# Attention output transposed in PSUM, the first convolution norm placed inside the attention, probabilities scaled before they are transposed

## The chip, the cores and the metric

The kernel runs on one core of a Trainium2 chip. Its engines are TensorE (PE, with PEld for its loads of weights), VectorE (DVE), ScalarE (ACT), GpSimd (POOL) and SyncE (SP), which issues the loads from memory. The metric is the device time of one execution in microseconds (us).

## The reference, cut to what matters

One layer of a decoder for a prompt of 1024 tokens and a sample group of 32 tokens (8 x 4), 1024 channels. What the change touches is the first part:

```python
q, k, v, a, gate = jnp.split(rms_norm(x, g_pre_mix) @ w_in, ...)
# 8 heads x 64; three dilated windows, combined by their softmax denominators
attn = combine_branches(outs, lses).reshape(B, T, 512)
c = causal_dwconv(a * sigmoid(gate), conv_w) + conv_b      # 512 channels, width 31
c = silu(layer_norm(c, ln_conv_g, ln_conv_b))              # the first norm of c
mix = concat([rms_norm(attn, g_out_attn), rms_norm(c, g_out_conv)])   # the second norm of c
x = x + rms_norm(mix @ w_out, g_post_mix)
```

Cross-attention into 256 memory tokens and a gated ConvFFN follow. All inputs and outputs are float32.

## The kernel before, in words

Activations are held transposed, channels on the partitions and 1056 tokens as columns, and the projections run over three tile columns of 352 tokens each, in the order 2, 0, 1 (CONV_ORDER). Each projection is a row of units: one unit is one weight tile of 1024 x 128 through one tile column. A weight tile is loaded by SP into one of four slots (`raw`), split by ACT into a high part (`whi`, `split_to`) and by DVE into a low part (`wlo`, `low_to`); three products of high and low parts make one float32 product. The output projection, the cross-attention's query and its output are the NX = 72 units of the loop over `t`; the first of them is the first unit spoken of below.

Each engine works through its queue in the order in which the program writes it; waits are on semaphores (`mark` counts up, `at` waits). The attention is a loop over steps s, the same on all engines. A step is a block of 128 queries i (0 to 7) and a pair of heads hp (0 to 3), 32 steps, i slowest, with (i + 1) x 128 keys. The three dilated windows are one softmax with a bias. A step is spread over the loop: `scores(s, 0)` and `maxima(s, 0)`, for more than 512 keys a second part, `negate(s)` and the exponentials `probabilities(s)` on ACT, in place in `Pp`; at s + 1 TensorE transposes the probabilities (`turn_p`), ACT copies them to `PT` (`turned`), and DVE takes the reciprocal of the sums (`shares`); at s + 2 TensorE multiplies (`product`) and DVE scales the result by the reciprocals into `ATT` (`attended`). Between them stand the slots of the sample group (`sample(g, r)`, three a step from s = 2 to 31, 44 for each of two groups of four batches): key tiles of the cache are transposed through bank 5 and multiplied (r = 0 to 27), a softmax, then four window products (r = 35, 37, 39, 41) on four groups of 32 columns of the array.

In the product, the transposed probabilities are the stationary operand (128 x 128) and V's columns of both heads the moving one; of each result one half is used:

```python
ins = mm(bank[4][:, e * P:(e + 1) * P], PT[:, e, blk * P:(blk + 1) * P],
         V[:, blk, hp * P:(hp + 1) * P], blk == 0, blk == i)
```

ATT has tokens on the partitions. Behind the attention stands the work between it and the output projection. For the convolution: means over channels by a matmul with ones (`conv_mean`), subtraction (`conv_centre`), squares (`conv_squares`), their mean (`conv_square_mean`), root (`conv_root`), reciprocal and scaling (`conv_scale`), silu, and squares, mean, root and scaling once more for the second norm. For the attention: sums of squares by row (`attention_square`), root, reciprocal, nine diagonal matrices DGA, and the transposition with scaling in one matmul (`turn_att`), before the first unit for tile column 2, behind units 0 to 3 for column 0 and behind units 8 to 11 for column 1. `mix_low` makes the high and low parts for the projection (`op_hi`, `op_lo`). The first weight tiles of the output projection are split partly at the end of the input projection and partly at step 24 (ACT) and 26 (DVE).

Of the kernel before, what the change touches and what calls it, by code (L numbers as in the profile page):

```python
# [130 lines left out]
def layout(nc, ctx, A, O, counts):  # L131
# [70 lines left out]
    DGA = [mn(f"DGA{i}", 61440 + 512 * i, [P, P]) for i in range(TT + 1)]  # L202
# [7 lines left out]
    ATT = mn("ATT", 20480, [P, TT + 1, AW])  # L210
# [9 lines left out]
    attsT = mn("attsT", 140288, [P, AT, NS])  # L220
# [17 lines left out]
    SQ = [mn(f"SQ{i}", 129024 + 1408 * i, [P, CW]) for i in range(4)]  # L238
    op_hi = [mn(f"op_hi{i}", 67584 + 22528 * i, [P, NT, CW], F32R) for i in range(2)]
# [148 lines left out]
    def y_free(eng, name, c):  # L388
# [3 lines left out]
        if (name, c) == ("out", 0):  # L392
            eng.wait_ge(*at("csq_used", 2 * CH * CT - 1))
        elif (name, c) == ("out", 1):
# [166 lines left out]
    def _(act):  # L561
# [136 lines left out]

        def sample(g, r):

            if 0 <= r < GROUP and on_scalar(g * GROUP + r):
# [37 lines left out]
        def attention_square(i):  # L739
            n = P if i < TT else NS  # L740
            if i == 0:
                act.wait_ge(*at("cst_out", BD - 1))
            else:
                act.wait_ge(*at("ass", i - 1))
            act.wait_ge(*at(*(("att", (AT * i + AT - 1, 1)) if i < TT else ("att8", 0))))
            act.activation(junk[0:n, :], ATT[0:n, i, :], ACT.Square, accum_out=ssx[0:n, i, 0:1]).then_inc(*mark("ass", i))
# [22 lines left out]
        for i in range((LAST_STEP - 6) // 4 + 1, TT):  # L769
            attention_square(i)  # L770

        attention_square(TT)
        act.wait_ge(*at("ass", TT))
        act.activation(rx2[:, 0:9], ssx[:, 0:9, 0], ACT.Sqrt, bias=eps[:, :], scale=1.0 / AW).then_inc(*mark("asd", 0))

        def conv_squares(second, j):
            c = CONV_ORDER[j]
            for k in range(CT):
                n = (second * CH + j) * CT + k
                act.wait_ge(*at("cs" if second else "cc", (c, k)))  # L780
                if n >= 4:
                    act.wait_ge(*at("csq_used", n - 4))
                act.activation(SQ[n % 4][:, :], C[:, k, c * CW:(c + 1) * CW], ACT.Square).then_inc(*mark("csq", n))

# [1496 lines left out]
```

## Time and profile before

| | |
|---|---|
| median of 3 runs | 1888.34 us (1885.1 to 1892.19) |
| the profiled execution | 1887.06 us, its span 1885.3 us |
| mean granted clock of TensorE | 0.982 |
| PE busy | 1794.4 us, 95% of the span |
| DVE busy | 1104.6 us, 59% |
| ACT busy | 869.7 us, 46% |

The span goes from the first to the last instruction. The attention lies at about 336 to 591 us of it, the first unit of the output projection starts at 631.89 us. A busy TensorE in these tables may still be waiting for its own pipeline, since the ends of matmuls are modelled.

### The profile page before, as it was taken

What the parts mean: (1) busy time and instruction counts of PE and PEld (TensorE: products, weight loads), DVE (VectorE), ACT (ScalarE), POOL (GpSimd) and SP (SyncE); (2) the same over time, 40 slices, a digit from 0 to 9 for tenths busy, and PEclk for the clock granted to TensorE, in tenths of its full rate; (3) what the DMA queues carried; (4) which work ended last, traced back from release to release, by engine and by line L of the source; (5) the groups of instructions that cost most, each with busy time, mean ns of one, the idle gap of its engine ahead of it and who ended that gap; (6) DMA issues with size and microseconds to landing.
All of it is one profiled execution on the core that took longest, in us unless ns stands there. A gap on an engine that the chain in (4) does not pass through costs nothing.

```text
span 1885.3 us, 30869 instructions
## 1 busy us (share of the span) xinstructions
PE 1794.4 (95%) x12354; PEld 1667.8 (88%) x12354; DVE 1104.6 (59%) x2055; ACT 869.7 (46%) x1647; POOL 0.9 (0%) x10
## 2 busy tenths in 40 slices
PE   7999999789998799999999898999999999999998
PEld 7999999556776689898877898999999999999998
DVE  5499993344445547753456756764467543576633
ACT  6322222244445456655445645544454543555533
POOL 0000000000000000000000000000000000000000
PEclk9999999899999799999999999999999999999999
DMA  7132122335231145444444333444444544444543
GB/s 234 56 122 80 56 91 91 141 125 190 79 119 51 36 122 162 147 142 129 134 145 124 105 108 112 134 134 139 141 135 134 165 131 138 135 140 140 152 138 101
DMA packets 349220, 233.76 MB, mean 124 GB/s; under 512 B 7979, under 2 KB 322465, under 8 KB 349071
## 3 DMA queue, kind: packets, MB, share of 16 engines
q1 hardware_dynamic: 342907, 220.24, 38.5%
q10 hardware_dynamic: 6172, 11.55, 1.7%
q8 instruction: 99, 1.62, 0.4%
q14 instruction: 42, 0.34, 0.1%
HBM read 220.68 MB, written 11.50 MB: 123 GB/s over the span
## 4 chain that ended last, share of the span: by engine, by line
PE 84%; DVE 7%; ACT 6%; issue 2%; DMA 1%; ACTq 0%; SPq 0%; DVEq 0%
PE bank L1134 78%; PE bank L1131 6%; ACT whi L570 1%; DVE wlo L1721 1%; DVE op_lo L1708 1%; DVE Y L1708 1%; ACT wide L584 1%; DVE op_x L2036 1%; DVE cv L1708 1%; DVE XT L2033 0%; ACT KTS L706 0%; DVE Sx L2021 0%; DVE KTS L1886 0%; DMA raw<-in_w_out_dram 0%; DMA stage_p<-in_ln_conv_b_dram 0%
## 5 line engine op out<-in xcount | busy, mean ns | idle before, releaser
L1134 PE MATMUL bank<-op_hi,whi 128*128 128x352 f32 x1632 | 542.8, 333 | 5.8 <-ACT Y L866 2.3
L1134 PE MATMUL bank<-op_hi,wlo 128*128 128x352 f32 x1632 | 528.3, 324 | 0.0
L1134 PE MATMUL bank<-op_lo,whi 128*128 128x352 f32 x1632 | 527.7, 323 | 0.0
L1721 DVE TENSOR_TENSOR wlo<-raw,whi 128x1024 fp32r<-128x1024 f32 (+1 forms) x312 | 373.6, 1200 | 260.0 <-ACT whi L570 259.4
L570 ACT ACTIVATE whi<-raw 128x1024 fp32r<-128x1024 f32 (+1 forms) x312 | 325.2, 1043 | 301.8 <-PE bank L1134 102.9
L1134 PEld LDWEIGHTS bank<-op_hi,whi 128*128 128x128 f32 x1632 | 309.9, 190 | 15.1 <-issue 10.5
L1134 PEld LDWEIGHTS bank<-op_lo,whi 128*128 128x128 f32 x1632 | 311.3, 191 | 0.3
L1134 PEld LDWEIGHTS bank<-op_hi,wlo 128*128 128x128 f32 x1632 | 309.7, 190 | 0.0
L1134 PE MATMUL bank<-fhi,whi 128*128 128x352 f32 x528 | 171.2, 324 | 0.0
L1134 PE MATMUL bank<-fhi,wlo 128*128 128x352 f32 x528 | 170.8, 323 | 0.0
L1134 PE MATMUL bank<-h1hi,whi 128*128 128x352 f32 x480 | 157.2, 327 | 3.0 <-DVE h1lo L1708 3.0
L1708 DVE SCALAR_TENSOR_TENSOR C<-U,cw,C 128x1024 f32<-128x1024 f32 x120 | 154.1, 1284 | 3.7
L1134 PE MATMUL bank<-h1hi,wlo 128*128 128x352 f32 x480 | 155.0, 323 | 0.0
L1134 PE MATMUL bank<-h1lo,whi 128*128 128x352 f32 x480 | 154.9, 323 | 0.0
L1134 PEld LDWEIGHTS bank<-fhi,wlo 128*128 128x128 f32 x528 | 99.8, 189 | 0.0
L1134 PEld LDWEIGHTS bank<-fhi,whi 128*128 128x128 f32 x528 | 99.4, 188 | 0.0
L1134 PEld LDWEIGHTS bank<-h1hi,whi 128*128 128x128 f32 x480 | 90.8, 189 | 3.1 <-DVE h1lo L1708 3.1
L1134 PEld LDWEIGHTS bank<-h1lo,whi 128*128 128x128 f32 x480 | 91.0, 190 | 0.0
L1134 PEld LDWEIGHTS bank<-h1hi,wlo 128*128 128x128 f32 x480 | 90.8, 189 | 0.0
L1134 PEld LDWEIGHTS bank<-V,PT 128*128 128x128 f32 x576 | 67.1, 192 | 22.0 <-issue 21.1
L1134 PE MATMUL bank<-flo_a,whi 128*128 128x352 f32 x264 | 84.9, 322 | 0.0
L1708 DVE SCALAR_TENSOR_TENSOR cv<-aext,fw,cv 128x352 f32<-128x352 f32 (+2 forms) x176 | 81.0, 491 | 3.9
(273 smaller groups left out, 2371.3 us busy)
## 6 DMA issues: line engine op xcount, KB each, us to landing
raw<-in_w_up_dram SPq DMA_DIRECT2D x132, 512.0 KB, 3.8
raw<-in_w_down_dram SPq DMA_DIRECT2D x48, 512.0 KB, 3.6
raw<-in_w_out_dram SPq DMA_DIRECT2D x24, 512.0 KB, 3.6
raw<-in_w_xq_dram SPq DMA_DIRECT2D x24, 512.0 KB, 3.6
raw<-in_w_xo_dram SPq DMA_DIRECT2D x24, 512.0 KB, 3.6
raw<-in_w_in_dram SPq DMA_DIRECT2D x20, 512.0 KB, 3.7
raw<-in_w_down_dram SPq DMA_DIRECT2D x24, 384.0 KB, 3.2
cached<-in_cache_win_k_dram SPq DMA_DIRECT2D x8, 1024.0 KB, 5.5
```

What stands on the lines that cost most here:

```text
L570: act.activation(whi[v % SLOTS][:, 0:nk, :], raw[v % SLOTS][:, 0:nk, :], ACT.Copy).then_inc(*mark("w_hi", v))
L584: act.activation(wide[0:n, :], src, ACT.Square, accum_out=ssx[0:n, i, 0:1]).then_inc(*mark("xss", i))
L1131: return pe.transpose(out, in_, ident[r:r + n, r:r + n])
L1134: return pe.matmul(out, lhsT, rhs, start=first, stop=last)
L1708: return dve.scalar_tensor_tensor(out=out, in0=in0, scalar=scalar, in1=in1, op0=op0, op1=op1)
L1721: dve.tensor_tensor(wlo[v % SLOTS][:, 0:nk, :], raw[v % SLOTS][:, 0:nk, :], whi[v % SLOTS][:, 0:nk, :].bitcast(F32), ALU.subtract).then_in ...
L2036: dve.tensor_tensor(op_x[SLOT[name, c]][:, m, :], XT[c][:, m, :], r[:, :], ALU.mult).then_inc(*mark("opx", (name, c, m)))
```

## The change

In the attention the operands of the product change places: V's 64 columns of one head are stationary, the transposed probabilities move, and the two heads write partitions 0 to 63 and 64 to 127 of one bank, in turn for each block. The output has channels on the partitions. So the reciprocals can no longer be applied to it by row; DVE multiplies the probabilities in place instead, after the next step's first maxima, and the transposes wait for that. ATT becomes [128, 4, 1056], the sample's outputs go straight into its last 32 columns, and the row sums, the diagonals and `turn_att` go. The attention's norm is now made like the convolution's: squares on ACT, mean by ones on TensorE, root on ACT, reciprocal and scaling on DVE, for tile column 2 ahead of the first unit, for the others behind units 2 and 3.

The first norm of the convolution moves into sample slots: means and centring into group 0's slots r = 29 to 34, squares, square means, roots and scaling into group 1's r = 28 to 35, all through bank 5. Its buffers SQ1, STD1 and RSC1 lie in the high halves of the four weight slots. So no weight tile of the output projection is split until step 30 (ACT) and 31 (DVE), where all four are.

```diff
+    halves = [place(f"half{i}", RING + 8192 * (i // 2) + 4096 + 1408 * (i % 2), [P, CW]) for i in range(8)]
+    SQ1, STD1, RSC1 = halves[0:4], halves[4:6], halves[6:8]
...
-            split_to(u + 3)
+            split_to(min(u + 3, LAST_IN))
...
+            if g == 1 and r - GROUP - 2 in (0, 2, 4):
+                conv_root(0, (r - GROUP - 2) // 2)
+            if g == 1 and r - GROUP in (0, 2, 4):
+                conv_squares(0, (r - GROUP) // 2)
...
-            if s >= 6 and (s - 6) % 4 == 0:
-                attention_square((s - 6) // 4)
...
-            if s == NP - 8:
+            if s == NP - 2:
                 split_to(XFIRST + 3)
...
+        def att_squares(j):
+            c = CONV_ORDER[j]
+            act.wait_ge(*at("att", NP - 1))
+            act.wait_ge(*at("satt", (1, 3, 1)))
+            for k in range(AT):
+                n = j * AT + k
+                if n >= 4:
+                    act.wait_ge(*at("asq_used", n - 4))
+                act.activation(SQA[n % 4][:, :], ATT[:, k, c * CW:(c + 1) * CW], ACT.Square).then_inc(*mark("asq", n))
+
+        def att_root(j):
+            act.wait_ge(*at("asq_used", j * AT + AT - 1))
+            if j:
+                act.wait_ge(*at("ars", j - 1))
+            act.activation(STDA[:, :], bank[5 - j % 2][:, 0:CW], ACT.Sqrt, bias=eps[:, :]).then_inc(*mark("asd", j))
+
         conv_silu(0)
         conv_squares(1, 0)
+        att_squares(0)
         conv_silu(1)
         conv_silu(2)
+        att_root(0)
         conv_root(1, 0)
...
-                pe.wait_ge(*at("pexp", (s, e)))
+                pe.wait_ge(*at("pn", (s, e)))
                 take(2 + e, "pt", (s, part, e))
...
-            take(4, "att", (s, 1))
+            take(4, "att", s)
             for e in range(2):
                 pe.wait_ge(*at("pt", (s, parts_of(i) - 1, e)))
-                for blk in range(i + 1):
-                    ins = mm(bank[4][:, e * P:(e + 1) * P], PT[:, e, blk * P:(blk + 1) * P], V[:, blk, hp * P:(hp + 1) * P], blk == 0, blk == i)
+            for blk in range(i + 1):
+                for e in range(2):
+                    h = 2 * hp + e
+                    ins = mm(bank[4][64 * e:64 * e + 64, 0:P], V[:, blk, h * DH:(h + 1) * DH], PT[:, e, blk * P:(blk + 1) * P], blk == 0, blk == i)
...
+            if g == 0 and r - GROUP in (1, 3, 5):
+                conv_mean((r - GROUP) // 2)
+            if g == 1 and r - GROUP in (1, 3, 5):
+                conv_square_mean(0, (r - GROUP) // 2)
...
+        def att_mean(j):
+            b = 5 - j % 2
+            take(b, "asd", j)
+            for k in range(AT):
+                n = j * AT + k
+                pe.wait_ge(*at("asq", n))
+                mm(bank[b][:, 0:CW], ones_c[:, :], SQA[n % 4][:, :], k == 0, k == AT - 1).then_inc(*mark("asq_used", n))
...
-            if t in range(AT):
-                turn_att(0, t)
-            if t - 8 in range(AT):
-                turn_att(1, t - 8)
+            if t in (2, 3):
+                att_mean(t - 1)
...
+            if g == 0 and r - GROUP - 2 in (0, 2, 4):
+                conv_centre((r - GROUP - 2) // 2)
+            if g == 1 and r - GROUP - 3 in (0, 2, 4):
+                conv_scale(0, (r - GROUP - 3) // 2)
...
             dve.reciprocal(prden[:, s % 2, :], pden[:, s % 2, :]).then_inc(*mark("prd", s))
+            dve.wait_ge(*at("prd", s))
+            n = (STEPS[s][0] + 1) * P
+            for e in range(2):
+                dve.tensor_scalar(Pp[s % 2][:, e, 0:n], Pp[s % 2][:, e, 0:n], prden[:, s % 2, e:e + 1], None, ALU.mult).then_inc(*mark("pn", (s, e)))
...
-                dve.tensor_scalar(ATT[:, i, h * DH:(h + 1) * DH], bank[4][:, e * P + e * DH:e * P + e * DH + DH], prden[:, s % 2, e:e + 1], None, ALU.mult).then_inc(*mark("att", (s, e)))
+            dve.tensor_copy(ATT[:, hp, i * P:(i + 1) * P], bank[4][:, 0:P]).then_inc(*mark("att", s))
 
         for s in range(LAST_STEP + 1):
             if s < NP:
                 maxima(s, 0)
+            if 0 <= s - 1 < NP:
+                shares(s - 1)
             if 0 <= s - 2 < NP:
                 attended(s - 2)
             sample(*sample_slot(s, 0))
-            if 0 <= s - 1 < NP:
-                shares(s - 1)
...
-            if s == NP - 6:
+            if s == NP - 1:
                 low_to(XFIRST + 3)
...
+        def att_scale(j):
+            c = CONV_ORDER[j]
+            dve.wait_ge(*at("asd", j))
+            dve.reciprocal(RSCA[j][:, :], STDA[:, :]).then_inc(*mark("ars", j))
+            dve.wait_ge(*at("ars", j))
+            for k in range(AT):
+                cols = ATT[:, k, c * CW:(c + 1) * CW]
+                dve.tensor_tensor(cols, cols, RSCA[j][:, :], ALU.mult).then_inc(*mark("an", (c, k)))
+
+        att_scale(0)
         conv_scale(1, 0)
...
-            if t - 1 in range(AT):
-                mix_low(0, t - 1)
+            if t in (2, 3):
+                att_scale(t - 1)
+            if t in (3, 4):
+                for k in (0, 1):
+                    mix_low(0, 2 * (t - 3) + k)
```

`mix_low` reads ATT in place of bank 4 or 5, as it reads C.

## Rows read from the trace of the kernel before

**Rows 1.** Page, part 4: the chain that ended last, by engine

```profile
PE 84%; DVE 7%; ACT 6%; issue 2%; DMA 1%; ACTq 0%; SPq 0%; DVEq 0%
```

**Rows 2.** Windows: length, busy us of PE, PEld, DVE, ACT, POOL, clock, DMA

```profile
370.00:380.00 10.00, 8.18 (x86) 5.43 (x79) 4.61 (x15) 3.97 (x14) 0.00 (x0) 1.00 0.21 60
560.00:590.80 30.80, 29.83 (x328) 24.62 (x327) 9.76 (x40) 15.53 (x29) 0.00 (x0) 1.00 0.13 46
590.80:631.90 41.10, 27.63 (x94) 17.71 (x92) 29.13 (x54) 25.76 (x51) 0.00 (x0) 0.76 0.18 58
666.00:672.00 6.00, 6.00 (x31) 5.92 (x29) 1.25 (x2) 0.61 (x2) 0.00 (x0) 0.72 0.42 109
```

**Rows 3.** The costliest group of 336 to 591 us: count, busy, mean ns

```profile
L1134 PE MATMUL bank<-V,PT 128*128 128x128 f32 x576 | 73.2, 282 | 2.5 <-ACT PT L737 2.5
```

**Rows 4.** Timeline of a late step: start us, duration us, engine, line

```profile
562.08 1.13 ACT L729 ACTIVATE Pp<-Pp,pneg 128x1024 f32<-128x1024 f32 x1
...
562.20 1.13 PE L1134 MATMUL bank<-KT,QT 64*128 64x512 f32 x4
...
563.26 3.84 PE L1134 MATMUL bank<-V,PT 128*128 128x128 f32 x32
...
566.94 1.04 PE L1131 MATMUL bank<-ident,Pp 128*128 128x128 f32 x8
...
568.96 1.74 PE L1134 MATMUL bank<-cached,PTS 128*32 128x128 f32 x56
...
569.74 0.75 DVE L1712 CUSTOM_DVE_ANT_0 Pp<-bank,wt,pmx 128x512 f32<-128x512 f32 x1
...
570.63 0.42 PE L1134 MATMUL bank<-V,PTS 32*32 32x128 f32 x8
...
570.98 1.09 PE L1131 MATMUL bank<-ident,Pp 128*128 128x128 f32 x8
...
572.00 1.13 PE L1134 MATMUL bank<-KT,QT 64*128 64x512 f32 x4
```

**Rows 5.** Timeline from the attention's last steps to the first unit

```profile
586.32 1.09 ACT L737 ACTIVATE PT<-bank 128x512 f32<-128x512 f32 x2 [0.32 <-PE bank L1131]
...
590.71 0.60 PE L1131 MATMUL bank<-ident,attsT 128*32 128x128 f32 x4
...
591.15 7.26 PE L1134 MATMUL bank<-C,ones_c 128*128 128x352 f32 x24
...
605.00 1.64 ACT L783 ACTIVATE SQ<-C 128x352 f32<-128x352 f32 x4
...
613.98 4.67 ACT L797 ACTIVATE C<-C,prm 128x352 f32<-128x352 f32 x8
...
618.66 1.28 ACT L790 ACT_TABLE_LOAD   x1
...
620.54 2.35 DVE L1983 RECIPROCAL RSC<-STD 128x352 f32<-128x352 f32 x1 [4.91 <-ACT STD L790]
622.93 1.83 DVE L1987 TENSOR_TENSOR C<-C,RSC 128x352 f32<-128x352 f32 x4
...
631.89 0.63 PE L1134 MATMUL bank<-op_hi,whi 128*128 128x352 f32 x1 [1.85 <-DVE op_lo L1708]
```

**Rows 6.** Groups of VectorE in the whole span, by shape

```profile
L1721 DVE TENSOR_TENSOR wlo<-raw,whi 128x1024 fp32r<-128x1024 f32 x288 | 350.7, 1220 | 246.3 <-ACT whi L570 245.6
...
L1997 DVE TENSOR_SCALAR DGA<-ident,rx 128x128 f32<-128x128 f32 x9 | 1.8, 277 | 0.0
...
L1903 DVE TENSOR_SCALAR Ps<-Ps,rden 128x928 f32<-128x928 f32 x2 | 1.4, 703 | 0.1
```

**Rows 7.** Timeline of TensorE behind the first unit; in brackets the wait

```profile
653.53 0.91 PE L1134 MATMUL bank<-DGA,ATT 128*128 128x128 f32 x6 [1.41 <-DVE op_lo L1708]
...
665.68 0.46 PE L1131 MATMUL bank<-ident,xtok 64*128 64x64 f32 x4 [2.53 <-DVE op_lo L1708]
```

**Rows 8.** The same at the ninth unit

```profile
685.70 1.41 PE L1134 MATMUL bank<-DGA,ATT 32*128 32x32 f32 x8
```

More of the change, by code:

```diff
@@ L811, in mix_low @@
             s = SLOT["mix", c]
[L812 to L813 removed]
+            act.wait_ge(*at("an", (c, m)))
+            act.activation(op_hi[s][:, m, :], ATT[:, m, c * CW:(c + 1) * CW], ACT.Copy, scale=g_of("g_out_attn", m)).then_inc(*mark("op_hi", ("mix", c, m)))
             act.wait_ge(*at("cf", (c, m)))
@@ L1362, in window_product, with conv_mean, conv_square_mean @@
             ins.then_inc(*mark("spv", b))
+        def conv_mean(j):
+            c = CONV_ORDER[j]
+            pe.wait_ge(*at("conv", "end"))
+            take(5, "cc", (c, CT - 1))
+            for k in range(CT):
+                ins = mm(bank[5][:, 0:CW], ones_c[:, :], C[:, k, c * CW:(c + 1) * CW], k == 0, k == CT - 1)
+            ins.then_inc(*mark("cmean", c))
+        def conv_square_mean(second, j):
+            b = (6, 1, 0)[j] if second else 5
+            take(b, "csd", second * CH + j)
+            for k in range(CT):
+                n = (second * CH + j) * CT + k
+                pe.wait_ge(*at("csq", n))
+                mm(bank[b][:, 0:CW], ones_c[:, :], (SQ if second else SQ1)[n % 4][:, :], k == 0, k == CT - 1).then_inc(*mark("csq_used", n))
         def sample(g, r):
+            if g == 0 and r - GROUP in (1, 3, 5):
+                conv_mean((r - GROUP) // 2)
+            if g == 1 and r - GROUP in (1, 3, 5):
+                conv_square_mean(0, (r - GROUP) // 2)
             if r == 0:
@@ L1596, in key_rows @@
             ins.then_inc(*mark("mkx_t", (mt, hf)))
-        for m in range(AT):
-            if m == 2:
-                conv_square_mean(1, 0)
-            turn_att(2, m)
+        conv_square_mean(1, 0)
+        att_mean(0)
         for t in range(NX):
@@ L1877, in _, with conv_centre, conv_scale @@
         dve.wait_ge(*at("tables", "s"))
+        def conv_centre(j):
+            c = CONV_ORDER[j]
+            dve.wait_ge(*at("cmean", c))
+            for k in range(CT):
+                cols = C[:, k, c * CW:(c + 1) * CW]
+                dve.tensor_tensor(cols, cols, bank[5][:, 0:CW], ALU.subtract).then_inc(*mark("cc", (c, k)))
+        def conv_scale(second, j):
+            c, n = CONV_ORDER[j], second * CH + j
+            dve.wait_ge(*at("csd", n))
+            r = RSC[:, j, :] if second else RSC1[n % 2][:, :]
+            dve.reciprocal(r, (STD if second else STD1)[n % 2][:, :]).then_inc(*mark("crs", n))
+            dve.wait_ge(*at("crs", n))
+            for k in range(CT):
+                cols = C[:, k, c * CW:(c + 1) * CW]
+                dve.tensor_tensor(cols, cols, r, ALU.mult).then_inc(*mark("cf" if second else "cn", (c, k)))
         def sample(g, r):
+            if g == 0 and r - GROUP - 2 in (0, 2, 4):
+                conv_centre((r - GROUP - 2) // 2)
+            if g == 1 and r - GROUP - 3 in (0, 2, 4):
+                conv_scale(0, (r - GROUP - 3) // 2)
             if 0 <= r < GROUP and not on_scalar(g * GROUP + r):
@@ L2138, in _ @@
                 conv_scale(1, t + 1)
-            if t - 1 in range(AT):
-                mix_low(0, t - 1)
+            if t in (2, 3):
+                att_scale(t - 1)
+            if t in (3, 4):
+                for k in (0, 1):
+                    mix_low(0, 2 * (t - 3) + k)
             if t - 8 in range(AT):
```

124 lines of the change are left out of this document (25 added, 99 removed).

## The prediction

> **What bounds the kernel now.** First I read the chain that ended last: 84% of it is TensorE's work [rows 1]. So time is won where TensorE waits or where its own work shrinks, and an edit on VectorE or ScalarE costs something only where TensorE ends up waiting for it. Then the windows. The attention runs from 336 to 590.7 us. Early in it TensorE is 82% busy (8.18 of 10 us from 370), in its last 30.8 us 97%. Behind it comes the hole that this change is about: from 590.8 to 631.9 us TensorE is busy 27.6 of 41.1 us, at a mean granted clock of 0.76, before the first unit of the output projection starts [rows 2]. The groups of the attention show the product of PT and V as TensorE's largest work there, 576 records [rows 3]. The timeline of a late step shows the order: first scores, product, transposes, second scores, sample work, transposes, and from one step's first scores to the next's it is 572.00 - 562.20 = 9.80 us [rows 4].
>
> **The product, values stationary.** 32 records take 566.94 - 563.26 = 3.68 us until the next instruction starts, 0.115 us each [rows 4]; 576 of them are 66 us. The number of records and their 128 moving columns stay the same, but each now fills only 64 columns of the array, the lower and the upper 64 in turn. Nothing in the trace has that shape. Two rows are near. 56 records of the sample's window product, on four groups of 32 columns in turn, take 570.63 - 568.96 = 1.67 us, 0.030 each, a quarter of 0.115: groups of columns run side by side, even into one bank. And four score records of 512 columns, on the two halves of the rows in turn, take 563.26 - 562.20 = 1.06 us [rows 4], where a record of 352 columns alone takes 0.293 (below), so four of 512 in a row would take 1.7. So I take half of 0.115: 33 us instead of 66, a gain of 33.1. The other bound is 0.115, no gain, and beyond it the 0.282 of a record by itself [rows 3].
>
> The handover from the 32-column products to the full transposes (570.63, then 570.98, with 8 records between) shows no gap [rows 4], so I take nothing for the change of shape. The Trainium skill (TensorEngine Tiling (Array Packing), Key Properties) says that changing the tiling mode drains the engine. By the row the sum stays as it is, by the rule it is the drain among the rivals.
>
> **The convolution norm, moved into the attention.** Three means and three square means, 24 records of 352 columns each, leave the hole. 24 take 7.26 us less the last one's tail of 0.2, 0.293 each [rows 5], so 48 of them bring TensorE +14.1 us. With the product that makes -33.1 + 14.1 = -19.0 us of TensorE's work in the attention. DVE gets 12 subtractions, 12 multiplications and three reciprocals of 2.35 us; ACT gets 12 squares and three roots. A root needs another table than the exponentials, each load takes 1.28, so up to six loads or 7.7 us of ACT [rows 5].
>
> **The probabilities scaled on DVE, in place.** Each step gets two multiplications of (i + 1) x 128 columns. Rows of that form are 277 ns at 128 columns and 703 at 928, so 754 at 1024, and 33 us of busy time over the 64. Upper bound for 1024: the 1220 of an operation with two tensors [rows 6]. In return two small multiplications of the output become one copy. DVE is 32 to 46% busy in the attention [rows 2], so its sum costs nothing; the order does. The transposes of step s now wait for exponentials, reciprocal and scaling. The chain of a step at i = 7: two exponentials 2.3 us, two scalings 1.4, the second head's transposes 0.5, second scores 1.06, two maxima 1.4, and about 1.4 for the accumulator reads, the reciprocal, the negation and seven handovers: 8.1 us [rows 4, 6]. TensorE's own work in such a step falls from 9.8 to 8.0 us. So the two are even, and from there a shorter product gives nothing.
>
> **What of the 19 us shows.** I laid the orders of the queues side by side with these durations. Steps 0 to 11 (i = 0 to 2): the product gives 4 x 0.23 x 6 = 5.5 us, but TensorE already waits there, and the longer way through DVE (0.15 + 2 x 0.3 us a step) takes it all: 0. Steps 12 to 15: -3.7 for the product, +7.05 for the means, +2.7 since bank 5 is held until DVE has centred four tiles and the sample's key transposes queue behind it: +6.0. Steps 16 to 23: 10.1 on paper, 8.3 kept. Steps 24 to 27: -6.4, +7.05, and +3 for TensorE waiting on squares and roots behind table loads: +3.7. Steps 28 to the end: -7.4, and +4.0 since the splitting of the first four weight tiles (ACT a little less, DVE 1.22 us each [rows 6]) now stands in the last two steps, ahead of the last exponentials and the last scaling: -3.4. Sum -2.0 us. Bounds: -19 if every wait hides; +12 if a scaling takes 1.22 us, when the chain is 9.1 us a step.
>
> **The hole.** Now: 590.71 to 631.89, 41.2 us. After, counted from the end of the last product: ACT is free 3.3 us before (587.41), loads a table (1.28), applies silu to one tile column (half of 4.67; ends at +0.4), squares it (1.64, +2.0), squares the attention's (1.64, +3.7), silu for two columns (4.67, +8.4), loads the root's table (1.28, +9.7), root (+10.1). DVE: reciprocal 2.35 and four multiplications 1.83 for the attention (+14.3), the same for the convolution (+18.5), eight low parts at 0.46 as the multiplications (+22.2), and 1.8 for the first ACT copies and the handovers: 24 us [rows 5]. Gone are the first conv passes, nine diagonals and the transposing matmuls. Gain 41.2 - 24.0 = 17.2 us. TensorE still stands idle ahead of the first unit, so that unit's slow start stays (a record of 0.63 us at 631.89) [rows 5].
>
> **Behind the hole.** The transposes of the attention for the other two tile columns go: four times 0.8 us (6 records) and four times 1.3 (8 records), 8.4 us [rows 7, 8]. Two attention means come: 2 x 2.3 = 4.6. Their waits go too: 1.41 us at 653.53 and 2.53 at 665.68, and behind the latter the granted clock is 0.72 for 6 us, 1.7 us lost [rows 2, 7]. Together 3.8 + 3.9 + 1.7 = 9.4. ACT's two roots now hold its queue for TensorE's means after the third and fourth unit, and the copies and splits behind them, so I keep 7.0. The low parts are due at the ninth unit and come some 7 us ahead of it.
>
> **Sum.** -2.0 - 17.2 - 7.0 = -26.2 us. The profiled execution took 1887.06 (span 1885.3), 1.3 below the median of 1888.34, so 1862 us.
>
> **Rivals.**
> Product without overlap: the two halves of the columns run one after another at 0.115. For it: no row has the shape. Against: both neighbours overlap. The attention then grows by the 14.1 of the conv and some 7.4 of waits, +21.5 instead of -2.0: 1886 us, no change.
> Halves that wait for each other, the case on the other side: if the weights of one half can't be loaded while the other half runs, a record costs more than 0.115. The sum is zero near 0.119 and slower by 0.5% (9.4 us) from 0.135; at the 0.282 of a record by itself it is 1886 + 576 x 0.167 = 1982 us. Against it: with four groups of columns the loads hide [rows 4].
> The clock: TensorE will wait 1 to 2 us several times a step at the end of the attention. The granted clock fell behind the pause of 2.53 us at 665.68, yet held at 1.00 with 82% busy from 370 [rows 2, 7]. Half clock for 20 us costs 10: 1872.
> A drain at each product: the rest of a record by itself, 0.282 - 0.115 = 0.17 us, once more a step than now, 32 x 0.17 = 5 us: 1867.
> A dearer scaling: at 1.22 us the attention grows 12 us instead of shrinking 2: 1876.
>
> **Chances.** Likeliest 0.62, its own range 1850 to 1871; clock 0.10; drain 0.05; scaling 0.08; no overlap 0.09; halves waiting 0.06. Range 1849 to 1880. Less than 0.5% (9.4 us) can't be told from no change: faster 0.82, same 0.12, slower 0.06.
>
> **What would show it.** Product records 0.058 us apart; the last product ending near 589; 24 us from there to the first unit; transposes waiting for DVE's Pp; no matmul reads ATT as weights. It is wrong if the records stay 0.115 apart, if the granted clock is 0.50 inside the attention, or if the conv work holds the sample work up by more than 10 us.

## The result, and the profile after

The changed kernel took 1868.36 us (median of 4 runs, 1866.86 to 1871.51) against 1886.87 us of the kernel before on the same chip (median of 4; the 1888.34 further up is that of the first three): ratio 0.9899, 95% interval 0.9874 to 0.9924. The forecast was 1862 us, range 1849 to 1880. The profiled execution's span is 1867.3 us, 18.0 below that of before.

The chain that ended last, by engine, in the changed kernel's page (beside [rows 1]):

```profile
PE 83%; DVE 8%; ACT 5%; issue 3%; DMA 1%; ACTq 0%; SPq 0%; DVEq 0%
```

Windows of the changed kernel, columns as in [rows 2]; the second is the attention's end, the third the hole:

```profile
412.00:450.00 38.00, 29.86 (x392) 20.52 (x393) 17.66 (x55) 10.95 (x27) 0.00 (x0) 0.91 0.48 165
560.00:595.50 35.50, 28.91 (x408) 20.21 (x396) 21.41 (x56) 23.45 (x40) 0.00 (x0) 1.00 0.24 83
595.50:619.30 23.80, 5.09 (x19) 3.01 (x17) 12.54 (x20) 17.24 (x34) 0.00 (x0) 0.72 0.29 100
666.00:672.00 6.00, 6.00 (x44) 5.96 (x43) 1.75 (x2) 2.83 (x8) 0.00 (x0) 1.00 0.37 106
```

TensorE was 97% busy at the end of the attention before, and is 81% busy there now (28.91 of 35.5 us). The hole has shrunk from 41.1 to 23.8 us. The slow stretch at 666 us is gone. The stretch from 412 us had 35.30 us of TensorE's work and a clock of 1.00 before; now it has 29.86 and 0.91.

The product as a group, and a late step on the timeline (beside [rows 3, 4]):

```profile
L1144 PE MATMUL bank<-PT,V 128*64 128x128 f32 x576 | 38.8, 279 | 2.8 <-ACT PT L761 2.8
```

```profile
567.78 1.13 PE L1144 MATMUL bank<-KT,QT 64*128 64x512 f32 x4
568.84 1.97 PE L1144 MATMUL bank<-PT,V 128*64 128x128 f32 x32
571.17 1.32 PE L1141 MATMUL bank<-ident,Pp 128*128 128x128 f32 x8 [0.36 <-DVE Pp L1966]
572.42 1.13 PE L1144 MATMUL bank<-KT,QT 64*128 64x512 f32 x4
...
577.58 1.97 PE L1144 MATMUL bank<-PT,V 128*64 128x128 f32 x32
```

32 records take 1.97 us with the last one's tail of some 0.2, so 0.057 us each: the two column halves run side by side. The mean duration is the same as before (279 against 282 ns), and yet the busy time has fallen from 73.2 to 38.8 us: what halved is the distance between records, not the time one spends in the engine. The transposes now wait for DVE's `Pp`.

From the last product to the first unit (beside [rows 5]):

```profile
593.63 1.97 PE L1144 MATMUL bank<-PT,V 128*64 128x128 f32 x32 [0.78 <-ACT PT L761]
...
600.19 4.66 ACT L788 ACTIVATE C<-C,prm 128x352 f32<-128x352 f32 x8
604.87 1.28 ACT L805 ACT_TABLE_LOAD   x1
606.16 0.55 ACT L805 ACTIVATE STDA<-bank,eps 128x352 f32<-128x352 f32 x1
...
606.82 2.35 DVE L1995 RECIPROCAL RSCA<-STDA 128x352 f32<-128x352 f32 x1 [10.88 <-ACT STDA L805]
...
619.28 0.63 PE L1144 MATMUL bank<-op_hi,whi 128*128 128x352 f32 x1 [16.58 <-DVE op_lo L1708]
```

The last product ends at 595.5, not at 589 as forecast; the first unit follows 23.8 us later, forecast 24.0. The wait to read here is DVE's 10.88 us for STDA: ACT sits on two columns of silu ahead of the root.

What TensorE waits for inside the attention, changed kernel, 402 to 600 us; columns: what waits, for what, us in total, times, longest:

```profile
PE bank L1141 <- DVE Pp L1966: 6.4, 7, 1.8
PE bank L1144 <- ACT half L710: 3.7, 2, 2.3
...
PE bank L1144 <- DMA cached<-in_cache_win_v_dram: 2.6, 1, 2.6
...
PE bank L1144 <- DVE C L1884: 1.5, 1, 1.5
```

None of the first, second and fourth were there before; the third was 1.2 us.

### The profile page after: what moved, and what is told of

Its sections match the earlier page's. It is cut to its first block, busy times and chain, and to the rows that moved or that the text cites. A ratio compares the mean times of both kernels' runs of the same rounds, so it can differ in the third digit from the quotient of the medians.

```text
span 1867.3 us, 30727 instructions
## 1 busy us (share of the span) xinstructions
PE 1757.9 (94%) x12286; PEld 1623.9 (87%) x12286; DVE 1134.5 (61%) x2091; ACT 876.4 (47%) x1648; POOL 0.9 (0%) x10
## 4 chain that ended last, share of the span: by engine, by line
PE 83%; DVE 8%; ACT 5%; issue 3%; DMA 1%; ACTq 0%; SPq 0%; DVEq 0%
PE bank L1144 77%; PE bank L1141 6%; DVE wlo L1721 1%; ACT whi L574 1%; DVE op_lo L1708 1%; DVE Y L1708 1%; DVE XT L2035 1%; ACT wide L588 1%; DVE Sx L2023 1%; DVE op_x L2038 0%; ACT KTS L730 0%; ACT Pp L753 0%; DVE KTS L1907 0%; DVE Sy L2016 0%; DVE Pp L1966 0%
## 5 line engine op out<-in xcount | busy, mean ns | idle before, releaser
L2016 DVE TENSOR_TENSOR Sy<-Sy,SQy 128x352 f32<-128x352 f32 x63 | 33.0, 523 | 79.3 <-ACT SQy L834 79.3
```

The source lines that it names most:

```text
L2016: dve.tensor_tensor(Sy[:, :], Sy[:, :], SQy[:, :], ALU.add).then_inc(*mark("ysum", (name, c, m)))
```

## The experiments

Every kernel is taken apart by three marks of TensorE's timeline: the first scores (near 338 us), the start of the last product, and the first unit. The two stretches between them (the last product counts to the hole here), and what follows the first unit ("rest"), are in the table, in us; what lies ahead of the first scores, 336 to 339 us, is left out; "ratio" is to the kernel before on the same chip.

| | attention | hole | rest | median | ratio |
|---|---|---|---|---|---|
| before | 249.8 | 44.8 | 1253.4 | | 1 |
| changed | 255.8 | 25.7 | 1248.0 | 1868.36 | 0.9899 |
| changed, again | 253.5 | 25.7 | 1247.2 | 1868.25 | 0.9901 |
| heads in turn | 262.1 | 25.7 | 1248.2 | 1875.03 | 0.9941 |
| conv norm behind | 241.3 | 45.4 | 1249.9 | 1876.14 | 0.9943 |
| scaling ahead | 255.3 | 25.7 | 1248.3 | 1868.08 | 0.9904 |
| split in pauses | 250.9 | 25.7 | 1250.2 | 1866.70 | 0.9894 |
| silu behind roots | 254.9 | 22.2 | 1249.1 | 1864.93 | 0.9885 |
| centring at once | 250.7 | 25.7 | 1250.1 | 1866.35 | 0.9890 |
| three together | 251.4 | 22.2 | 1246.0 | 1862.09 | 0.9871 |
| unscaled | 248.4 | 25.7 | 1248.7 | 1862.21 | 0.9858 |
| unscaled, conv behind | 229.6 | 45.4 | 1248.6 | 1862.72 | 0.9859 |
| three, scaled on GpSimd | 355.8 | 22.3 | 1250.7 | 1969.02 | 1.0428 |
| three, scaling ahead | 256.0 | 22.9 | 1248.0 | 1864.60 | 0.9876 |

The rest spreads from 1246 to 1251 over kernels that are the same there, and the attention by 2.3 us between two executions of the same kernel: smaller differences in one row say nothing. The hole repeats to 0.15 us wherever ACT's order there is the same, except in the last kernel.

The attention once more, cut at the first scores of steps 12, 16, 24 and 28; its last stretch ends where the last product starts:

| | to step 12 | 12 to 15 | 16 to 23 | 24 to 27 | from 28 |
|---|---|---|---|---|---|
| before | 73.2 | 26.5 | 67.3 | 37.4 | 45.5 |
| changed | 71.7 | 36.8 | 60.0 | 42.3 | 45.0 |
| changed, again | 70.5 | 35.5 | 61.0 | 40.9 | 45.5 |
| conv norm behind | 69.0 | 29.7 | 61.7 | 37.7 | 43.3 |
| split in pauses | 70.6 | 33.8 | 60.0 | 40.9 | 45.6 |
| centring at once | 71.5 | 32.5 | 60.0 | 40.9 | 45.8 |
| unscaled | 70.2 | 37.3 | 58.1 | 42.1 | 40.6 |
| unscaled, conv behind | 69.2 | 30.1 | 58.8 | 32.6 | 39.0 |

**Heads in turn.** The product's records no longer alternate between the column halves.

```diff
-            for blk in range(i + 1):
-                for e in range(2):
+            for e in range(2):
+                for blk in range(i + 1):
```

> The changed kernel, but the product runs all blocks of one head and then all of the other, so that neighbouring matmuls use the same 64 columns. Theory (overlap of the two halves is what shortens the product): its 576 records are about 0.115 us apart in place of 0.057, 33 us more of TensorE's work, of which the waits of the step absorb a third: 20 to 28 us slower than the changed kernel, so 0 to 0.5% slower than before. Rival (the steps are bound by the chain exponentials, scaling, transposes, not by the product): records 0.115 apart, yet at most 8 us slower than the changed kernel. Second rival (64 columns are faster by themselves): records stay below 0.08 us apart and the time does not move.

Ratio 0.9941 (0.9925 to 0.9958), about 7 us above the changed kernel. The group and four products of this kernel:

```profile
L1144 PE MATMUL bank<-PT,V 128*64 128x128 f32 x576 | 58.3, 279 | 2.9 <-ACT PT L761 2.9
```

```profile
376.94 0.66 PE L1144 MATMUL bank<-PT,V 128*64 128x128 f32 x8
...
409.50 1.14 PE L1144 MATMUL bank<-PT,V 128*64 128x128 f32 x12
...
561.56 2.89 PE L1144 MATMUL bank<-PT,V 128*64 128x128 f32 x28
...
572.57 3.33 PE L1144 MATMUL bank<-PT,V 128*64 128x128 f32 x32
```

Four records more cost 0.44 us, 0.11 each. In the changed kernel it is 0.22 us (1.75 for 28, 1.97 for 32), 0.055 each, and before it was 0.45 (3.39 and 3.84). So in long products the pitch does come from alternating; without it each further 64-column record costs what a full one does. In short products the order makes no difference: 8 records, four of one half and then four of the other, take 0.66 us here and 0.66 in the changed kernel, against 1.16 before. From 12 records on (six of one half in a row) this kernel falls behind, 1.14 against 0.88. So the products' busy time is only 19.5 us longer, where the theory had 33, and the median of the time only 6.7. The theory that 20 to 28 us would come through fell, and the rival's size (at most 8 us) holds: a part of the slower product filled TensorE's waits; those for `Pp` fell from 6.4 to 2.7 us. Only steps 16 to 23 let it through: from the product of step 16 to that of step 24 it takes 66.5 us instead of 60.9, where the products' own rows say 6.6.

**Conv norm behind the attention**, with its splitting of the weights, as in the kernel before. What stays of the change is the product, the scaling and the attention's norm.

```diff
-            if g == 0 and r - GROUP in (1, 3, 5):
-                conv_mean((r - GROUP) // 2)
-            if g == 1 and r - GROUP in (1, 3, 5):
-                conv_square_mean(0, (r - GROUP) // 2)
...
+        for j in range(CH):
+            conv_mean(j)
+        for j in range(CH):
+            conv_square_mean(0, j)
```

> The changed kernel with the first convolution norm back behind the attention and the weight tiles of the output projection split as before; product, scaling and the attention's norm stay as changed. My theory (moving the norm costs inside the attention about what it saves in the hole, since it holds up the sample slots, brings half clock and table loads): the attention ends 17 to 23 us earlier, near 575 us, the hole grows from 24 to 40 to 46 us, and the total is within 5 us of the changed kernel. Rival (the hole is free time and filling it is the gain): the attention ends less than 12 us earlier and the total is 8 us or more above the changed kernel. Second rival (the move was a loss): the total is 5 us or more below the changed kernel.

Ratio 0.9943 (0.9928 to 0.9958), 8 us above the changed kernel. The hole is 19.7 us longer, the attention 12 to 15 us shorter. So the move buys 19.7 us of hole for 12 to 15 of attention. Neither expectation fits: the theory had the total within 5 us of the changed kernel, and the rival, whose total (8 us or more) came, had the attention end less than 12 us earlier, where it ended 14 us earlier (at 581.5).

This run also shows the longest wait for the scaled probabilities. A step with the window softmax on its timeline:

```profile
522.41 2.35 DVE L1720 TENSOR_TENSOR wlo<-raw,whi 128x1024 fp32r<-128x1024 f32 x2
...
523.41 1.75 PE L1143 MATMUL bank<-PT,V 128*64 128x128 f32 x28
...
524.68 0.68 DVE L1711 CUSTOM_DVE_ANT_0 Ps<-bank,ws 128x512 f32<-128x512 f32 x1
...
526.48 0.69 DVE L1711 CUSTOM_DVE_ANT_0 Pp<-bank,wt 128x512 f32<-128x512 f32 x1
...
527.91 1.28 DVE L1961 TENSOR_SCALAR Pp<-Pp,prden 128x896 f32<-128x896 f32 x2
528.65 1.97 PE L1140 MATMUL bank<-ident,Pp 128*128 128x128 f32 x8 [3.49 <-DVE Pp L1961]
```

The exponentials were done at 524.7. DVE first has the low parts of two weight tiles (`wlo`, to 524.7), then the window's maxima (`Ps`), then the next step's, then the reciprocal and the scaling, and only then can TensorE transpose: 3.49 us of wait. The low parts stand here because in this kernel the weights are split at steps 24 and 26; in the changed kernel they are not, and its longest wait for `Pp` is 1.8 us. The eight transposes then take 1.97 us where 1.04 is usual [rows 4]: TensorE came out of the pause at half its clock, and the granted clock was 0.64 from 525 to 535 us.

**Scaling ahead of the next step's first maxima.**

```diff
-            if s < NP:
-                maxima(s, 0)
             if 0 <= s - 1 < NP:
                 shares(s - 1)
             if 0 <= s - 2 < NP:
                 attended(s - 2)
+            if s < NP:
+                maxima(s, 0)
```

> The changed kernel with the scaling of a step's probabilities ahead of the next step's first maxima. Theory (with the shorter product the chain of a step and TensorE's work are even, so whatever DVE puts into the chain shows): the first maxima, 1.3 us, now wait for the exponentials and stand between them and the second maxima; 8 to 20 us slower than the changed kernel, with larger waits of TensorE for Pp and of the scores for the maxima. Rival (TensorE's own work bounds the steps): within 3 us of the changed kernel.

Ratio 0.9904 (0.9889 to 0.9918), as the changed kernel. The theory of 8 to 20 us more fell; the time is that of the rival. The waits of 402 to 600 us:

```profile
PE bank L1144 <- DMA cached<-in_cache_win_v_dram: 6.0, 2, 4.3
...
PE bank L1141 <- DVE Pp L1966: 3.6, 2, 3.0
```

The waits for `Pp` fell from 6.4 to 3.6 us, and the wait for the load of the window of values grew from 2.6 to 6.0. That load is issued when the window product before it has freed the buffer, and the loads of the windows take 5.3 to 7.6 us from issue to landing in the changed kernel (405 to 450 us); whoever reaches it sooner waits longer.

**Weights split behind the last steps**, not in them.

```diff
-            if s == NP - 2:
+            if s == NP - 1:
                 split_to(XFIRST + 3)
...
-            if s == NP - 1:
-                low_to(XFIRST + 3)
...
+        low_to(XFIRST + 3)
         dve.memset(eps_d[:, :], EPS / (D * D)).then_inc(*mark("eps_d", 0))
```

> The changed kernel with the four weight tiles split by ACT behind the last exponentials (step 31) and by DVE behind the attention, in place of ACT at step 30 and DVE ahead of the last scaling. Theory (the splits stand in the chain of the last two steps): ACT's 3.9 us ahead of the copies of step 30 go, 1.5 us ahead of the last copies come, DVE's 0.9 us ahead of the last scaling go, and DVE's lows fall into its pause of 10.9 us in the hole: 2 to 4 us faster than the changed kernel. Rival (the last steps are bound by TensorE's own work): no difference.

Ratio 0.9894 (0.9879 to 0.9909): 1.7 us under the changed kernel by the medians, which the intervals don't tell from none. The attention is 2.6 to 4.9 us shorter, but not where the edit acts: from step 28 on it takes 45.6 us, against 45.0 and 45.5 in the changed kernel. What is shorter lies ahead of step 24, above all in steps 12 to 15, where this execution kept its clock (1.00 from 412 to 450 us). So the theory of 2 to 4 us fell; the runs show no gain from this edit.

**The changed kernel once more, and three single edits beside it on one chip.**

> The changed kernel once more, as the measure for the three beside it on the same chip. Expected 0.9899 of the kernel before, within 0.15%, and the attention's last product ending about 595.5 us, the first unit at about 619 us.

It took 1868.25 us, ratio 0.9901 (0.9888 to 0.9915); the last product ends at 595.9 us, and the first unit starts at 617.9.

**Silu behind the roots.**

```diff
         att_squares(0)
-        conv_silu(1)
-        conv_silu(2)
         att_root(0)
         conv_root(1, 0)
+        conv_silu(1)
+        conv_silu(2)
```

> ScalarE's silus of the second and third conv chunk (two of the eightfold groups of 4.66 us in the hole) go behind the two square roots that DVE waits for (10.88 us idle for STDA in the changed kernel). Theory that ScalarE's order sets the hole: the root comes 4 to 5 us earlier, the first unit starts 19 to 20 us after the last product instead of 23.8, and the time falls by 3 to 5 us (an extra table load of 1.28 us lies behind). Rival, that the units behind need the silued conv as soon as the attention's norm is done: the first unit starts early but the conv half of op_lo comes late, and the time is the same within 1 us.

Ratio 0.9885 (0.9871 to 0.9900), 3.3 us under the kernel beside it. The wait for the root and what follows, on its timeline:

```profile
598.67 1.28 ACT L805 ACT_TABLE_LOAD   x1
...
601.76 2.35 DVE L1995 RECIPROCAL RSCA<-STDA 128x352 f32<-128x352 f32 x1 [7.45 <-ACT STDA L805]
...
614.22 0.63 PE L1144 MATMUL bank<-op_hi,whi 128*128 128x352 f32 x1 [13.15 <-DVE op_lo L1708]
```

DVE waits 7.45 us in place of 10.88, and the hole is 3.5 us shorter: 20.3 from the end of the last product. The theory's 3 to 5 us holds, at its lower end: the root comes 3.4 us earlier, not 4 to 5, since it now waits 1.15 us for TensorE's mean.

**Centring at once.** A chunk is centred in the sample slot of its mean, and its bank is free for the next.

```diff
+            if g == 0 and r - GROUP - 1 in (0, 2, 4):
+                conv_centre((r - GROUP - 1) // 2)
...
-            if g == 0 and r - GROUP - 2 in (0, 2, 4):
-                conv_centre((r - GROUP - 2) // 2)
```

> VectorE's centring of a conv chunk moves one sample slot up, to the slot in which its mean is made, so that the next mean no longer waits for its bank (1.46 us in the changed kernel, followed by a stretch at the lower clock). Theory that this wait and its clock are part of what the attention lost in steps 12 to 15: that stretch shortens by 2 to 3 us and the time falls by as much. Rival, that the load of the values' window (issued when its buffer comes free, 7.6 us later there) is the floor of these steps: the wait for that load grows by what the centring wait gives back, and the time is the same within 1 us.

Ratio 0.9890 (0.9877 to 0.9904), 1.9 us under the kernel beside it. The wait of 1.5 us for `C` is gone and the attention is shorter by 2.8; the sizes point to the theory, the intervals overlap. Steps 12 to 15 take 32.5 us, 3.0 to 4.3 less than in the changed kernel. About 1.3 of this is the edit: in the split run, which has the pause but kept its clock behind it, they take 33.8. The rest is the clock, which was 1.00 from 412 to 450 us here too. The rival fell: the wait for the load didn't grow (2.3 us, with 2.6 and 3.7 in the changed kernel).

**The three together.**

> The split of the later weights pulled out of the last steps (as in the fourth run, 1.7 to 2.6 us), the silus behind the roots and the centring a slot earlier, all in one kernel. If they act in different places they add up: 6 to 10 us under the changed kernel, about 1859 to 1862 us. Rival, that they overlap (the split and the silus both want ScalarE in the hole): 3 to 5 us.

1862.09 us, ratio 0.9871 (0.9854 to 0.9888): 6.2 us under the changed kernel beside it, the lower edge of what adding up would give (1.7 + 3.3 + 1.9 = 6.9). This beats both kernels. The hole is 3.4 us shorter, the attention 2.1, the rest 1.2. Since the split alone showed no gain of its own, this does not show that three gains add up.

**Unscaled.** DVE's two multiplications a step are left out and the transposes wait for the exponentials; so the attention's output is not normalised in this kernel and the next.

```diff
-                pe.wait_ge(*at("pn", (s, e)))
+                pe.wait_ge(*at("pexp", (s, e)))
...
-            n = (STEPS[s][0] + 1) * P
-            for e in range(2):
-                dve.tensor_scalar(Pp[s % 2][:, e, 0:n], Pp[s % 2][:, e, 0:n], prden[:, s % 2, e:e + 1], None, ALU.mult).then_inc(*mark("pn", (s, e)))
```

> The changed kernel with VectorE's scaling of the probabilities left out (32 pairs of up to 1.42 us); the turns wait for the exponentials alone. This leaves a part of the computation out. Theory that the product's halved time went to waits for the scaled probabilities (7.3 us in 8 waits) and to VectorE's longer order in each step: the attention ends 8 to 14 us earlier than in the changed kernel, and the time falls by 8 to 12 us. Rival, that TensorE waits in these steps for something else (window loads, the conv group's roots): less than 4 us.

**Unscaled, conv norm behind.** The edits of this one and of the second run together.

> As the run before, and with the first conv norm behind the attention as it was before the change: what is left in the attention is the transposed product alone. The scaling is left out of the computation here too. The second run had the last product start 7.4 us before the kernel before's and end 9.3 us before it, with the scaling in. Theory that the product alone would give what the prediction took (19 us after the waits that take some of its 33): the last product ends 16 to 22 us before that of the kernel before. Rival, that even without the scaling the steps are bound by maxima, exponentials and copies: 9 to 12 us.

The first took 1862.21 us, ratio 0.9858 (0.9829 to 0.9887), the second 1862.72, ratio 0.9859 (0.9834 to 0.9883). Together with the changed kernel and the second run they make a square, the length of the attention in us:

| | conv norm behind | conv norm inside |
|---|---|---|
| unscaled | 229.6 | 248.4 |
| scaled | 241.3 | 253.5, 255.8 |

Against the 249.8 of before, the product and what goes with it (one copy for two scalings of the output, no row sums) give 20.2 us. The scaling takes back 11.7 of them without the conv norm, 5 to 7 with it; the conv norm costs 18.8 without the scaling, 12 to 15 with it. So neither has a price of its own. The first expectation was 8 to 14 us for the attention and 8 to 12 for the time, and 5 to 7 came, with 6 by the medians and 8 by the ratios; the second was 16 to 22, and 20.2 came. Without the scaling the two places of the conv norm take the same time (0.9858 and 0.9859): 18.8 us of attention for 19.7 of hole. With the scaling the move pays 8 us.

Why it pays there is only argued. The blocks put the whole difference into steps 24 to 27: the conv norm costs 9.5 us in them without the scaling (42.1 against 32.6) and 3.3 to 4.6 with it. That it lies in the waits that the scaling has already made is one reading. But the splitting of the weights moves with the conv norm, whose buffers lie in the weight slots: where the norm is behind, DVE's low parts stand in step 26, ahead of the scaling, and they and the half clock after them are in the 37.7 us of these steps. No run has the norm behind and the split elsewhere, so the two are not told apart.

The unscaled kernel with the conv norm behind also shows what stays in the way of a faster product. A window product on its timeline:

```profile
434.37 3.21 PE L1143 MATMUL bank<-cached,PTS 128*32 128x128 f32 x56 [4.87 <-DMA cached<-in_cache_win_v_dram]
```

In the kernel before this wait was 1.2 us long. Behind it 56 records take 3.21 us instead of 1.74: half the clock again.

**Two attempts to make the scaling cheaper**, both on top of the three edits. First on GpSimd:

```diff
+        for s in range(NP):
+            n = (STEPS[s][0] + 1) * P
+            pool.wait_ge(*at("prd", s))
+            for e in range(2):
+                pool.tensor_scalar(Pp[s % 2][:, e, 0:n], Pp[s % 2][:, e, 0:n], prden[:, s % 2, e:e + 1], None, ALU.mult).then_inc(*mark("pn", (s, e)))
```

> The kernel of the three edits together (ratio 0.9871 to the kernel before), with the scaling of the probabilities on GpSimd, which has no work in the attention, in place of VectorE. The two runs without scaling ended the attention 7 us (conv norm inside) and 11 us (conv norm behind) earlier. Theory that it is VectorE's order that makes the scaling dear: if GpSimd needs under 1.5 us for 1024 columns, the transposes wait less and the time falls by 3 to 6 us more. Rival, that a GpSimd pass over 1024 float32 columns takes 2 us or more, or slows VectorE's own passes beside it: the waits for the scaled probabilities grow, 2 us each in the 16 longest steps, and the time is 10 to 40 us above.

1969.02 us, ratio 1.0428 (1.0406 to 1.0449), 107 us above the three together, far beyond even the rival. Groups of GpSimd, and TensorE's first wait from 336 to 700 us:

```profile
L566 POOL TENSOR_SCALAR Pp<-Pp,prden 128x1024 f32<-128x1024 f32 x8 | 22.7, 2843 | 39.2 <-DVE prden L1967 39.2
...
L566 POOL TENSOR_SCALAR Pp<-Pp,prden 128x128 f32<-128x128 f32 x8 | 4.8, 614 | 297.2 <-DVE prden L1967 297.2
```

```profile
PE bank L1146 <- POOL Pp L566: 69.3, 56, 3.4
```

1024 columns take 2.84 us, which is within the rival's words; that the wait falls in every step (56 times) and the granted clock with it (0.82 to 0.86 from 336 to 690 us in windows of 66 to 100 us) is what its sum had left out. The Trainium skill (Trainium Architecture — The Big Picture, The five engines, in one table) calls GpSimd half as fast as VectorE for such streams; here it is 2843 against 750 ns at 1024 columns, 3.8 times. Then the order of the third run on top of the three edits:

> The three edits together and VectorE's scaling ahead of the next step's first maxima, as in the third run. Theory: that run ended the attention 2.5 us earlier than the changed kernel but gave 3.4 us to the wait for the values' window; with the centring moved up as well the two act in one place, so 0 to 2 us under the three edits. Rival, that the first maxima now come late in the steps in which VectorE is longest: 2 to 4 us above.

1864.60 us, ratio 0.9876 (0.9855 to 0.9896), 0 to 3 us above the three together; its wait for the window of values is 6.3 us in two. The order gains nothing here either.

## Why the prediction was right, and where it was off

**The product's halves** overlap as forecast: 0.057 us a record against 0.0575. The rival without overlap is out, and the case on the other side with it. The run with the heads in turn shows that in products of 12 records and more the order of the two loops makes it: there one half after the other costs 0.11 a record, as before.

**The change of shape.** From scores to product the shape changes in both kernels (1.06 us each, 567.78 to 568.84 against 562.20 to 563.26), so nothing can be read there. The place to look is behind the product, which had the shape of the transposes before and has it no more. The kernel before:

```profile
542.61 3.39 PE L1134 MATMUL bank<-V,PT 128*128 128x128 f32 x28
545.84 1.04 PE L1131 MATMUL bank<-ident,Pp 128*128 128x128 f32 x8
...
551.74 3.39 PE L1134 MATMUL bank<-V,PT 128*128 128x128 f32 x28
555.06 1.74 PE L1134 MATMUL bank<-cached,PTS 128*32 128x128 f32 x56
```

And the unscaled kernel with the conv norm behind, in which neither handover has a wait:

```profile
530.58 1.75 PE L1143 MATMUL bank<-PT,V 128*64 128x128 f32 x28
532.26 1.09 PE L1140 MATMUL bank<-ident,Pp 128*128 128x128 f32 x8
...
538.22 1.75 PE L1143 MATMUL bank<-PT,V 128*64 128x128 f32 x28
539.90 1.74 PE L1143 MATMUL bank<-cached,PTS 128*32 128x128 f32 x56
```

Before, the next work starts 3.23 us after the product if it has the same shape and 3.32 if it has another; now it is 1.68 in both cases, both being changes. So a change of shape costs 0.09 us, half of the 0.17 that the rival gave it, and by this at most 3 us in 32 steps (an estimate). The forecast took nothing for it. The Trainium skill (TensorEngine Tiling (Array Packing), Key Properties) says that changing the tiling mode drains the engine; what these rows show of it is the 0.09 us.

**The conv norm** was costed at +14.1 us of TensorE's time, and with the scaling in place the attention grew by 12 to 15 when it moved in. That this is near is partly luck: without the scaling it is 18.8, since the waits for roots and centring come on top.

**The scaling** takes 750 ns at 1024 columns (forecast 754):

```profile
L1966 DVE TENSOR_SCALAR Pp<-Pp,prden 128x1024 f32<-128x1024 f32 x8 | 5.7, 750 | 0.1
L1966 DVE TENSOR_SCALAR Pp<-Pp,prden 128x128 f32<-128x128 f32 x8 | 1.9, 283 | 0.1
```

The prediction's sentence that its sum costs nothing and its order does is right, and the chain of a step was close to even with TensorE's work, as said. But that balance was drawn for a step without the window softmax.

**The term that was off is the attention's -2.0 us.** It started 0.5 us later and ended 4.8 us later than before (595.5 against 590.7), so +4.3 came for it. The end is 6.8 us off, most of the 8.2 by which the sum missed. By blocks of steps (unrounded starts of the first scores at steps 12, 16, 24 and 28: 410.40, 436.86, 504.14, 541.55 before; 409.45, 446.24, 506.25, 548.59 after), forecast and measured: 0 and -1.5; +6.0 and +10.3; -8.3 and -7.3; +3.7 and +4.9; -3.4 and -2.2. Nearly two thirds of the miss lie in steps 12 to 15, where one pause was costed as a pause alone and others not at all:

```profile
406.89 2.63 PE L1144 MATMUL bank<-C,ones_c 128*128 128x352 f32 x8
...
412.51 0.88 PE L1141 MATMUL bank<-ident,Pp 128*128 128x128 f32 x6 [1.12 <-DVE Pp L1966]
414.85 4.29 PE L1144 MATMUL bank<-C,ones_c 128*128 128x352 f32 x8 [1.46 <-DVE C L1884]
...
432.08 1.09 PE L1141 MATMUL bank<-ident,Pp 128*128 128x128 f32 x8 [0.97 <-DVE Pp L1966]
...
442.96 3.00 PE L1144 MATMUL bank<-cached,PTS 128*32 128x128 f32 x56 [2.64 <-DMA cached<-in_cache_win_v_dram]
```

Against the forecast's -3.7 for the product, +7.05 for the means and +2.7 for bank 5, the rows of this block give: product -2.8; two groups of means +5.0, the first of the three lying ahead of step 12; the pause for the centring +1.5; two waits for the scaled probabilities +2.1, which the sum had at nothing; the longer wait for the load (2.64 against 1.17) +1.5, also at nothing; and half the clock behind two of the pauses, eight means in 4.29 instead of 2.60 us and the window product in 3.00 instead of 1.74, +3.0. Together that is the 10.3. That the load is a floor here shows with all else taken out: the block from the product of step 12 to that of step 16 is 33.9 us then, with 30.6 before.

In the other blocks errors met. Steps 0 to 11 were to give nothing, but without the group of means at 406.89 they are 4 us shorter than before, and so they are in both kernels with the conv norm behind: there the shorter product did show. From step 28 on the sum had +4.0 for the splitting of the weights; moving the split showed no gain there, and leaving the scaling out took 4.4 to 4.9 us off. So these runs show a price of the scaling in the last steps, which the sum had at nothing, and none of the splitting.

The half clock behind a short pause is not certain. In the second execution of the same kernel the first of the two stretches kept its clock (1.00 from 412 to 430 us), and so did the square means of steps 24 to 27 (1.00 from 520 to 540, with 0.94 in the first); its attention was 2.3 us shorter. But its last product ran at half the clock:

```profile
592.26 3.68 PE L1144 MATMUL bank<-PT,V 128*64 128x128 f32 x32 [0.78 <-ACT PT L761]
```

The rival on the clock had placed its loss at the attention's end. In the first execution the clock stayed at 1.00 there; in this one, and in five of the other kernels (last products of 3.4 to 3.7 us), it did not. In the changed kernel that cost nothing: the hole from the product's start is 25.7 us either way, and only DVE's wait for STDA is shorter, 9.17 us in place of 10.88, while ACT is at its silus.

One of the prediction's own signs of being wrong did come: the granted clock fell to half inside the attention, in both executions. The forecast of the time stood in spite of it, since in the first it lost 4.6 us (the 3.0 above, and the square means at 536.93 in 4.22 instead of 2.60 us) and not the 10 of the rival.

**The hole** was forecast at 24.0 and is 23.8, by the steps named: silu, table load, root, two reciprocals, eight multiplications, the copies. ACT was free 2.0 us ahead of the product's end and not 3.3 (its table load starts at 593.50), so the root came 1.1 us late; the 1.8 us kept for copies and handovers took that up.

**Behind the hole** -5.4 us came against -7.0. The slow stretch at 666 is gone as said; the rest of the difference, 1.6 us, is within what that part of the span spreads over equal kernels.

**The sum.** 0.5 from a later start, +4.3 attention, -17.4 hole, -5.4 behind it: -18.0 in the spans, where -26.2 was forecast. The product alone would give more than all of it (20.2 in the attention); the scaling, the conv norm, the window's load and the clock took it back there, and the hole paid for them.

What stays open: which part of the scaling's cost is wait and which is the clock that falls behind the wait; no run held the clock. The splitting of the weights was moved alone only once, and its effect is not told from none; with the conv norm behind the attention it was never moved, so how much of the square's interplay is its own is open too.

## What to carry to other kernels

A cut in the busiest engine's work is worth what the next chain of the same step leaves of it. Lay out that chain for the worst kind of step, not for the usual one, and look for a load whose buffer comes free late: the gain stops there. Where two edits go into one phase, test them as a square, since each can hide in the other's waits and then neither has a price of its own. Then cut the phase into blocks and see where the interplay lies: it may come from a third thing that moves along with one of them. The same cut tells whether a gain lies where the edit acts, or in a stretch whose clock happened to hold.

Work in an idle stretch that is a chain through several engines holds more time than its matmuls take (14.1 us of them held 19.7 us here). Whether moving it pays is decided by the waits that it finds where it goes.

## What the runs showed of the hardware

Two column halves of one bank, alternating, take 0.055 us for each further record of 128 float32 columns (1.75 for 28, 1.97 for 32). The same records one half after the other take 0.11 from 12 records on, and so did the full width; with 8 records, four to a half, the order makes no difference (0.66 us).

Going from one shape to another (128 x 128, 128 x 64, 128 x 32 of the array in use) between two matmuls costs 0.09 us: behind 28 records of full width the next start is 3.23 us away with the same shape and 3.32 with another.

GpSimd needs 2.84 us for a multiplication by a column scalar of 128 x 1024 float32 in place and 0.61 for 128 x 128; VectorE 0.75 and 0.28.

Behind a pause of 1.46 us TensorE ran at half its clock in one execution (eight means in 4.29 us) and at the full clock in the next (2.60 us).
